# The first FFN's second half with seven-product groups, and a pooling norm whose last squares TensorE sums by itself

## The reference, cut to what matters

```python
def swiglu(h, w_in, w_out):
    g, u = jnp.split(h @ w_in, 2, axis=-1)
    return (jax.nn.silu(g) * u) @ w_out

    cond = jax.nn.silu(c)
    for i in range(DEPTH):
        mod = (cond @ ada_w[i] + ada_b[i]).reshape(b_, N_SUBLAYERS, 3, D_MODEL)
        h = adaln(x, norm_g[i, 0], mod[:, 0, 0], mod[:, 0, 1])      # norm, scale, shift
        x = x + 0.5 * (1.0 + mod[:, 0, 2][:, None, :]) * swiglu(h, ffn_w_in[i, 0], ffn_w_out[i, 0])
        h = adaln(x, norm_g[i, 1], mod[:, 1, 0], mod[:, 1, 1])
        ...                                                          # pooling or attention
        x = x + (1.0 + mod[:, 1, 2][:, None, :]) * y
        h = adaln(x, norm_g[i, 2], mod[:, 2, 0], mod[:, 2, 1])
        x = x + 0.5 * (1.0 + mod[:, 2, 2][:, None, :]) * swiglu(h, ffn_w_in[i, 1], ffn_w_out[i, 1])
```

## Time and profile before

| | us |
|---|---|
| median of 3 runs (lowest to highest) | 2896.26 (2895.88 to 2897.73) |
| the profiled execution | 2896.0 |
| its span in the profile | 2893.6 |
| PE busy | 2873.8, 99% |
| DVE busy | 1939.4, 67% |
| ACT busy | 1264.7, 44% |
| POOL busy | 144.9, 5% |
| DMA, mean over the span | 127 GB/s |

### The profile page before, as it was taken

How to read it: one execution, slowest core, us unless ns; L and a number is a source line. 1 busy time by engine, 2 the same in 40 slices (tenths; PEclk the granted TensorE clock), 3 DMA queues, 4 the chain that set the end, 5 groups by cost and what they waited for, 6 DMA issues and landing times. The chain is left out here.

```text
span 2893.6 us, 40922 instructions
## 1 busy us (share of the span) xinstructions
PE 2873.8 (99%) x16099; PEld 2485.7 (86%) x16099; DVE 1939.4 (67%) x2624; ACT 1264.7 (44%) x1752; POOL 144.9 (5%) x297
## 2 busy tenths in 40 slices
PE   8999999999999999999999999999999999999999
PEld 7888889899898998868999988788888888888887
DVE  8667688777786777876856758766535467754453
ACT  4223255344452445474533445654414348443332
POOL 0111100100001001040000000200000001000000
PEclk9999999999999999999999999999999999999999
DMA  7867613524236243251332322413232222232231
GB/s 299 272 217 255 210 45 115 206 109 154 89 115 230 91 168 107 88 182 61 108 126 79 114 91 88 160 63 110 87 105 98 95 81 95 96 108 95 88 109 66
DMA packets 100944, 366.99 MB, mean 127 GB/s; under 512 B 11248, under 2 KB 11808, under 8 KB 100784
## 3 DMA queue, kind: packets, MB, share of 16 engines
q1 hardware_dynamic: 77616, 276.56, 27.9%
q0 software_dynamic: 23168, 88.17, 8.8%
HBM read 362.51 MB, written 2.18 MB: 126 GB/s over the span
## 5 line engine op out<-in xcount | busy, mean ns | idle before, releaser
L1263 DVE TENSOR_TENSOR wl<-raw,wh 128x1024 fp32r<-128x1024 f32 x393 | 477.1, 1226 | 519.4 <-ACT wh L697 518.9
L697 ACT ACTIVATE wh<-raw 128x1024 fp32r<-128x1024 f32 x393 | 409.8, 1054 | 752.4 <-PE PS L2131 685.1
L2131 PE MATMUL PS<-HH,wh 128*128 128x512 f32 x1560 | 608.2, 390 | 0.4 <-DVE HL L1979 0.3
L2131 PE MATMUL PS<-HL,wh 128*128 128x512 f32 x1560 | 607.7, 390 | 0.0
L2131 PE MATMUL PS<-HH,wl 128*128 128x512 f32 x1560 | 607.7, 390 | 0.0
L2131 PEld LDWEIGHTS PS<-HH,wh 128*128 128x128 f32 x1560 | 293.1, 188 | 62.1 <-DVE HL L1979 0.8
L2131 PEld LDWEIGHTS PS<-HH,wl 128*128 128x128 f32 x1560 | 293.0, 188 | 60.5
L2131 PEld LDWEIGHTS PS<-HL,wh 128*128 128x128 f32 x1560 | 293.1, 188 | 60.3
L2131 PE MATMUL PS<-AH,wh 128*128 128x512 f32 x848 | 330.7, 390 | 0.5 <-DVEq L2014 0.5
L2131 PE MATMUL PS<-AL,wh 128*128 128x512 f32 x848 | 330.5, 390 | 0.0
L2131 PE MATMUL PS<-AH,wl 128*128 128x512 f32 x848 | 330.3, 390 | 0.0
(11 more groups left out here) (346 smaller groups left out, 5107.6 us busy)
## 6 DMA issues: line engine op xcount, KB each, us to landing
raw<-in_stream SPq DMA_DIRECT2D x459, 512.0 KB, 3.4
acc<-in_stream POOLq DMA_DIRECT2D x54, 512.0 KB, 4.9
WK<-in_stream SPq DMA_DIRECT2D x42, 512.0 KB, 4.5
piece<-in_stream POOLq DMA_DIRECT2D x38, 512.0 KB, 5.0
WK<-in_stream POOLq DMA_DIRECT2D x24, 512.0 KB, 6.6
arena<-in_stream SPq DMA_DIRECT2D x16, 512.0 KB, 12.5
HT<-in_stream POOLq DMA_DIRECT2D x12, 512.0 KB, 6.8
TBa<-negcum POOLq DMA_DIRECT2D x8, 640.0 KB, 5.0
```

The lines of the kernel that those rows point to most:

```text
L697: F(wh[:, r, :], raw[:, r, :], ACT.Copy).then_inc(hi_done, 1)
L1263: TT(wl[:, r, :], raw[:, r, :], wh[:, r, :].bitcast(F32), ALU.subtract).then_inc(lo_done, 1)
L2131: mm = MM(PS[g % 2][:, j, :], l, x, start=(first and i == 0), stop=(last and i == 2), skip_group_check=after_halves)
```

## The change

FFN 0 gets five seven-product groups, its whole second half (`FAST[0] = (0, 5)`). What they need is made room for: the four input sums are made on DVE during groups 2 to 4 of the first half; in the first half only 30 modulation sums are done (six places), and 20 follow in its first down projection, three after each split, then 10 in the second; FFN 2 and FFN 3 take 24 and 10 each. The last six loads ahead of a seven-product part use only the places `piece` and `HT`, since `WK` must be free for the weights. FFN 0's 20 loads wait until the last input low part is made. `late_constants` goes behind the `add_out` of FFN 0's first half-step. `cond` is kept in `bands`, is copied by ACT to its old place when 60 sums are done, and only then does SP load the real `bands`.

In the pooling norm, the squares of half tiles (6, h) and (7, h) are no longer added by DVE: PE sums the added tile and these two separately into the same column, so `square_sums` has 6 matmuls per half for 2. DVE's order is rewritten with it, and the spreading of the first half's root moves from before the second-last to before the last pooled tile on PE.

```diff
-FAST = {2: (4, 5), 3: (4, 5), 5: (4, 5)}
-ADA_BY = {0: 8 + 3 * NADA, 2: 8 + 4 * NADA, 3: 8 + 5 * NADA}
-ADA_EARLY = ADA_BY[0]
-ADA_PHASES = (16, 8)
+FAST = {0: (0, 5), 2: (4, 5), 3: (4, 5), 5: (4, 5)}
+ADA_EARLY = 30
+ADA_PHASES = {0: (20, 10), 2: (24, 10), 3: (24, 10)}
+ADA_BY = {0: 60, 2: 94, 3: 128}
+ADA_PLACE = [2, 3, 0] + [4, 5, 6]
+def late_places():
+    places = []
+    for into_part, behind in ADA_PHASES.values():
+        places += [(0, 1, 2, 3)[i % 4] if i < into_part - 6 else i % 2 for i in range(into_part)]
+        places += [(0, 1, 2, 3)[i % 4] for i in range(behind)]
+    return places
...
+def ada_free(m):
+    earlier = [i for i in range(m) if ADA_PLACES[i] == ADA_PLACES[m]]
+    return max(earlier[-1] + 1, ADA_EARLY if m >= ADA_EARLY else 0) if earlier else 0
...
+def summed_apart(nm, k, h):
+    return nm["full"] == 0 and h is not None and k >= 6
...
-            sp.dma_start(bands[:, 0:NBAND], A["params"][:, NCOL:NCOL + NBAND]).then_inc(bands_in, 16)
...
+                if st is plan[2]:
+                    load_chunks(loaded, part["c"] + st["halves"][1][1] + 1)
+                    loaded = part["c"] + st["halves"][1][1] + 1
+                    sp.wait_ge(cond_moved, 1)
+                    sp.dma_start(bands[:, 0:NBAND], A["params"][:, NCOL:NCOL + NBAND]).then_inc(bands_in, 16)
...
-                for part, n in zip(st.get("parts", ()) if st.get("gate") in ADA_BY else (), ADA_PHASES):
-                    pl.wait_ge(a_ready, part["e"] + part["n"] + 1)
+                for part, n in zip(st["at"], ADA_PHASES[st["gate"]]) if st["kind"] == "ffn" and st["gate"] in ADA_BY else ():
+                    if part:
+                        pl.wait_ge(a_ready, part["e"] + part["n"] + 1)
+                    else:
+                        pl.wait_ge(mix_ready, 4)
                     for i in range(n):
-                        pl.wait_ge(ada_step, max(m - 3, ADA_EARLY))
...
+                        load_ada(m)
...
-                            if paired:
-                                late_constants()
...
-                                splits_with_sums(c + nt // 2 + RING, 2 if st["parts"] else 1, ada or at["ada"])
-                                if half == 1 and st["parts"]:
-                                    fast_groups(st, st["parts"][1],
+                                ahead = c + nt != c_last and st["at"][1]
+                                splits_with_sums(c + nt // 2 + RING, 3 if ahead else 2,
+                                                 0 if ada is None else ada - ADA_PHASES[st["gate"]][1] if ahead else ada)
+                                if half == 1 and ahead:
+                                    fast_groups(st, ahead,
                                                 lambda: add_out(st, g, c + nt // 2, 4, gate))
                                 else:
                                     add_out(st, g, c + nt // 2, 4 * half, gate)
+                                if st is plan[2] and half == 0 and ahead:
+                                    late_constants()
...
+                slots = [SUM_SLOT] + [square_slot(i) for i in apart]
                 for a in (2 * h, 2 * h + 1):
-                    mm = MM(ps[:, 2 + h, STAT + a:STAT + a + 1], WK[:, SUM_SLOT, 128 * a:128 * a + 128], ones[:, 0:1],
-                            start=True, stop=True, skip_group_check=True)
+                    for slot in slots:
+                        mm = MM(ps[:, 2 + h, STAT + a:STAT + a + 1], WK[:, slot, 128 * a:128 * a + 128], ones[:, 0:1],
+                                start=slot == slots[0], stop=slot == slots[-1], skip_group_check=True)
...
-                        if d == 6:
+                        if d == 7:
                             spread_root(nm, 0)
...
-    ffn(wi[0, 0], wo[0, 0], h1, paired=True)
+    ffn(wi[0, 0], wo[0, 0], h1, paired=True, fast=FAST[0])
```

More of the change, by code:

```diff
@@ L59 @@
 NADA = 24
-ADA_RING = 3
 FAST_SLOTS = 6
@@ L107, in x_parts, with squares_added @@
     return [(k, None) for k in range(full)] + [(k, h) for h in range(2) for k in range(full, KT)]
+def summed_apart(nm, k, h):
+    return nm["full"] == 0 and h is not None and k >= 6
+def squares_added(nm, i):
+    return sum(not summed_apart(nm, *p) for p in x_parts(nm)[1:i + 1])
 def h_parts(nm):
@@ L170, in make_plan @@
         elif kind == "ffn":
-            st["parts"], st["sets"] = [], sum(bool(p.get("parts")) for p in plan[:-1])
+            st["parts"], st["at"], st["sets"] = [], [None, None], sum(bool(p.get("parts")) for p in plan[:-1])
             for half, (ng, nt) in enumerate(f["halves"]):
@@ L179, in make_plan @@
                                             s=at["fs"] + add["fs"], f=at["fg"] + add["fg"], turn=-7 * nf % RING, slot=(8 - 4 * nf) % FAST_SLOTS,
-                                            tile=2 * (ng - nf), sums=ADA_BY[f["gate"]] - ADA_PHASES[1] if late else 0))
+                                            tile=2 * (ng - nf), sums=max(m + 1 for m in range(ADA_BY[f["gate"]] - ADA_PHASES[f["gate"]][1])
+                                                      if ADA_PLACES[m] in (2, 3)) if late else 0))
+                    st["at"][half] = st["parts"][-1]
                 add["fs"] += 7 * nf
@@ L397, in build @@
         ada0_in = [sem(f"ada0_in{i}") for i in range(8)]
-        ada_in = [sem(f"ada_in{i}") for i in range(ADA_RING)]
-        ada_late_in = [sem(f"ada_late_in{i}") for i in range(4)]
+        ada_in = [sem(f"ada_in{i}") for i in range(len(ada_tiles))]
         cond_moved = sem("cond_moved")
@@ L1006, in _ @@
                                 hidden_group(st, e + u, g + u, c + 4 * (u + 1), cv + u, j + u, 2 * u, 0)
+                            act.wait_ge(ada_step, ADA_EARLY)
+                            for i in range(4):
+                                mix_high(i, st["sets"])
                             e, cv, g, c, j, pairs = e + ng, cv + ng, g + ng, c + 4 * ng, j + ng, 0
@@ L1027, in _ @@
                                 split_until(c + nt // 2 + RING)
+                                if st is plan[2] and half == 0 and c + nt != c_last:
+                                    late_constants()
+                                if st is plan[2] and c + nt == c_last:
+                                    act.wait_ge(ada_step, ADA_BY[0])
+                                    F(condb, condc, ACT.Copy).then_inc(cond_moved, 1)
                             c += nt // 2
@@ L1801, in _ @@
-                        if ada and not st["parts"]:
-                            paired = st is plan[2] and c == st["c"]
-                            if paired:
-                                split_until(c + 10)
-                                hidden_group(st, e, g, cv, j, 0, 0)
-                                split_until(c + 11)
-                                hidden_group(st, e + 1, g + 1, cv + 1, j + 1, 2, 0)
-                                split_until(c + 12)
-                                e, cv, g, c, j = e + 2, cv + 2, g + 2, c + 8, j + 2
-                            for u in range(2 if paired else 0, ng):
+                                fast_groups(st, part, None)
@@ L1815, in _ @@
                                 hidden_group(st, e, g, cv, j, 2 * u, 0)
                                 e, cv, g, c, j = e + 1, cv + 1, g + 1, c + 4, j + 1
-                            ada_until(min(ada, at["ada"] + 1))
-                            if paired:
-                                late_constants()
-                        pairs = 0 if ada or st["parts"] else ng // 2
+                            for i in range(4):
+                                mix_low(i, sets)
+                        pairs = 0 if part or st is plan[2] else ng // 2
@@ L1828, in _ @@
                         e, cv, g, c, j = e + 2 * pairs, cv + 2 * pairs, g + 2 * pairs, c + 8 * pairs, j + 2 * pairs
-                        if ng % 2 and not ada and not st["parts"]:
+                        if ng % 2 and not part:
                             split_until(c + 4 + RING)
@@ L2541, in _ @@
                                 group(c, g, nt, a_tile, (lambda k: [(a_ready, e + k // 2 + 2)]),
-                                      begun=1 if half == 0 and st["parts"] else 0)
+                                      begun=1 if half == 0 and part else 0)
                             c, g = c + nt // 2, g + 1
```

186 lines of the change are left out of this document (110 added, 76 removed).

## The result

| | before | changed |
|---|---|---|
| median of 4 runs, us | 2896.38 (2895.88 to 2897.73) | 2920.96 (2917.68 to 2922.59) |
| span of the profiled execution | 2893.6 | 2920.4 |
| PE busy | 2873.8 | 2878.4 |
| DVE busy | 1939.4 | 1999.3 |

What follows compares the result with a forecast made beforehand. PE was taken as the bound, busy 2873.8 of 2893.6 us, its new work waiting on DVE's written order. Terms -8.0 + 10.0 + 1.0 + 5.0 + 1.0 = +9.0 gave 2905.3 us on the median's scale, range 2889 to 2913.

Steps and rivals of the forecast that it cites:

- Five groups: FFN 0's second half: five groups at 20.16 us each as seven products, for 21.76, saving 8.0 us.
- The wait in FFN 0: First down projection: PE waits 9.4 to 12.5 us for the late seventh split; taken as +10.0.
- T0: 149.32 us: ACT rounds the first chunk whose place comes free in FFN 0's first down projection; seventh split needed 54.4 later.
- The clock: Lower granted clock behind FFN 0's stall: between 0 and 1.7 us, taken as +1.0.
- FFN 2 and 3: PE waits 0.4 to 3.1 us for the third low part in each; taken as 2.5 each, +5.0 together.
- the walk: Step-by-step count of DVE's ordered work and POOL's loads in the down projections, giving when splits and low parts are ready.
- T': FFN 2's starting point for the same count, 535.7 us before the change; sum 24 expected at T' + 62 to 64.6.
- The pooling: Pooling norm: more records of ones and a longer rounded-tile wait, against fewer DVE adds; net +1.0 us, -0.5 to +2.
- B: Rival: only FFN 0 stalls, FFN 2 and 3 loads land in 4.6 us or less; 2895 to 2900 us, chance 0.22.
- C: Rival: each load lands in about 3.2 us, FFN 2 and 3 do not stall; 2892 us, chance 0.08.
- D: Rival: slack in DVE, ACT and POOL hides everything, only the -8.0 stays; 2888 us, chance 0.17.
- E: Rival, the slower end: landings of 6 us or a POOL pause passing to PE; +20, 2916 us, chance 0.05.

Runs made afterwards that it cites:

- e6: e5 plus six load places in all and FFN 0's seventh split ahead of the first half-step's add_out; 2889.45 us, ratio 0.9975.
- e2: Changed kernel with the late constants behind the first half-step of FFN 0's second down projection; 2916.91 us, ratio 1.0071.
- e1: Changed kernel with three places (PR, piece, HT) instead of two for the last six loads ahead of a seven-product part; 2913.73 us, ratio 1.0058.
- p1: Kernel before with 16 dummy DVE operations ahead of the add_out in FFN 0's first down projection; 2905.41 us, one execution.
- p2: Kernel before with 22 dummy DVE operations ahead of the add_out in FFN 0's first down projection; 2913.02 us, one execution.
- e10: Changed kernel with SP's first six weight loads of a second-half seven-product part waiting for all sums of the down projection; 2921.39 us.
- e8: Kernel before with the new pooling norm and nothing else, root moved; 2898.38 us, ratio 1.0007.
- e9: e8 with the root spread before the second-last pooled tile, as in the kernel before; 2896.36 us, ratio 1.0000.
- e4: Changed kernel with the pooling norm of before; 2922.45 us.
- e5: Changed kernel with four places for the last six loads, late constants in FFN 0's second down projection, and the old pooling norm; 2897.40 us.

## Why the prediction was right in kind and wrong in size

**Five groups, -8.0: right.** Without waits on splits and low parts (e6) the stretch is -8.0 to the tenth.

**The wait in FFN 0, +10.0 (9.4 to 12.5): right in sum, 11.5, by parts that partly made up for each other.** Right were: POOL's first load at T0 + 14.1 for 14.0, sum 12 done at T0 + 40.7 for 38.3 to 41.5. "Sum 15 needs its load issued behind sum 13: 0.4 + 4.6 + 1.15" was mis-sized: it took 8.3, the landing being 6.8, and the sixth split, which I had put inside the waits, came 3.9 late. The seventh ended at T0 + 68.6 for 63.8 to 66.9. e2 confirms the constants' 4.8 as part of it, e1 the two places.

**The clock, +1.0: mis-sized in FFN 0, and left out everywhere else.** I took "between 0 and 1.7" from the windows of the pooling and charged it once. FFN 0's two waits cost 4.5; the waits in FFN 2 and 3, for which I charged no clock at all, 1.4 and 1.5. p1 and p2 show 2.3 to 2.8 for a single wait in a stream of 512-column matmuls. "A stall of 10 us can only be worse" does not hold either: 13.44 us lost 2.3, the pooling's 1.65 up to 3.4. The price goes by the number of longer waits rather than by their microseconds, and four of them, besides the pooling's, had one: both of FFN 0's and the 3.06 of FFN 2 and of FFN 3.

**FFN 2 and 3, +2.5 each: the step that failed by most, 7.7 and 7.4, 10.1 of the 17.8 us missed.** The waits were 5.7 and 5.1 for 2.5 each, the clock 1.4 and 1.5 for nothing. Two things of the walk were too short. The first load of the last six took 8.0 us (POOL 590.91, sum 598.87 in the changed trace) for the 4.6 that I used, because SP's weight loads begin on the same event: the prediction counts POOL's loads alone and never asks what the freeing of `WK` triggers. e10 shows it. The last sum ended at T' + 66.0 (T' now 547.7, counted from the same event), for 62 to 64.6. And between it and the `add_out` stood ACT's rounding of the second weight, which I had left out: 613.76 to 620.77 is 7.0 for 5.7. In the changed kernel:

```profile
590.91 0.53 POOL L668 DMA_DIRECT2D piece<-in_stream  x1 [4.36 <-DVE mod L1393]
...
600.40 0.53 POOL L668 DMA_DIRECT2D piece<-in_stream  x1 [7.51 <-DVE mod L1393]
```

and DVE's sum of the first of these loads:

```profile
598.87 1.23 DVE L1393 CUSTOM_DVE_ANT_0 piece<-piece,bands 128x1024 f32<-128x1024 f32 x1 [3.04 <-DMA piece<-in_stream]
```

**The pooling, +1.0 (-0.5 to +2): +3.4 in this profile, 1.8 by itself (e8).** The term held its range by the median, not in the profile. The walk had the sums at about the same time; they start 0.95 earlier against the pooling's first add. It had the wait on the rounded tile grow from 0.81 to 1.5; it was 1.16, and e9 shows that it comes with the root's place. For the cold loss there, 2.8 more than before in this profile, the term had nothing; up to 1.8 of such a difference appears between profiles that have the same norm.

**The rivals.** B, C and D fell: all three took fewer or shorter waits. The landing of 3.2 us that the Trainium skill gives (DMA: Bandwidth & Descriptors, on the anatomy of one DMA from GpSimd) was not reached by any of the sums' loads in the changed kernel's FFN 0 (150 to 215 us): they took 3.4 to 8.8, with a median of 5.8; the 3.6 to the start of the sum in e10, at a DMA share of 0.44, comes near it. E, +20 "from landings over 5.5 on", was the nearest, by its condition too, and had a chance of 0.05; its 1.7 for the clock was too little as well. The sum of the terms as measured: -8.0 + 11.5 + 4.5 + 15.1 + 3.4 = 26.5 of 26.8.

What stays open: why the cold loss behind a wait is 1.4 in one case and 3.1 in another, and how much of the norm's cost is in the changed kernel's median, since e4 and e5 did not resolve it.

## What to carry to other kernels

Where one engine works in written order and feeds the bound engine, its slack can be used up by many small things together, and then each of them costs its full time: 4.8 us of small operations, hidden where they stood before, cost 4 us behind the last sums, and moving one split ahead of an `add_out` gained 6. Price each wait of TensorE of 2.5 us or more at its length plus about 2 us, the mean of this case, and count the waits. When buffers come free earlier or later, list everything that starts on that event on every queue; a burst on one queue lengthens the landings on which another queue's walk rests.

## What the runs showed of the hardware that I had not expected

A wait of 13.4 us cost no more in clock than one of 5.9 (2.3 and 2.6 us), and the same wait of 1.65 ahead of the same pooling lost 1.6 us in two profiles and 2.9 to 3.4 in five others: one profile does not give the price of a wait to within 1.5 us. A load of 512 KB by POOL, to the start of its sum, took 3.6 us at a DMA share of 0.44, and 6.8 and 8.0 while SP moved 3 MB.
